# Two transformer blocks on one core: products of a quarter taken kind by kind in the blocks after each norm

## The chip, the cores and the metric

The kernel runs on one NeuronCore of a Trainium2 chip. The metric is the device time of one execution in microseconds (us), as the median of several runs. All matrix data are float32; TensorE multiplies them in its float32r format.

## What is computed

Two transformer blocks over one sequence of 256 tokens with 1024 features. Cut to what matters here:

```python
def first_block(x, mem, ...):
    h = _rmsnorm(x, norm_mix_pre)
    x = x + _rmsnorm(_mixer_sublayer(h, ...), norm_mix_post)
    h = _rmsnorm(x, norm_mem_pre)
    x = x + _rmsnorm(_memory_cross_attention(h, mem, ...), norm_mem_post)
    h = _rmsnorm(x, norm_ffn_pre)
    return x + _rmsnorm(_swiglu(h, w_gate_up, w_down), norm_ffn_post)

def second_block(x, ...):
    for layer in range(2):
        if layer == 1: shared = nsa_shared_kv(h, kv_w, ...)
        h = post_norm(h, 0.5 * swiglu(h, ...), ...)
        mix = chunked_sgu_mixer(h, ...) if layer == 0 else nsa_mixer(h, shared, ...)
        h = post_norm(h, mix, ...)
        h = post_norm(h, 0.5 * swiglu(h, ...), ...)
```

So there are five SwiGLU feed-forward parts (width 2816), three mixers, and a norm between any two of them. Each norm needs the whole row of a token, so the next product cannot begin on a token before its norm is done.

## The kernel before

**Split in two parts.** For accuracy every operand of a weight product is kept as two float32r tiles: the rounded value (high part) and what rounding left (low part). A product of an activation tile and a weight tile is three matmuls into the same PSUM bank: high by high, high by low, low by high. `product` (L632) issues them one after another, so in the profile L634, L635 and L636 are the three kinds. In the token layout the stationary operand is `st_hi` or `st_lo` (128 features by 128 tokens) and the moving operand a row of `whi` or `wlo` (512 or 256 columns).

**Weights.** They stream through a ring of three slots of 1 MB, called units, as a fixed list. SyncE issues the loads into `raw`; ScalarE copies to `whi` (L1393, semaphore `whi_ready`); VectorE subtracts to `wlo` (L1939, `wlo_ready`), GpSimd for a few units (L2638). The first two units of the program are split by halves, with `half_hi_ready` and `half_lo_ready` for the first half (L1408, L2066). TensorE counts `w_used` when a unit is done, which frees its `whi` and `wlo`.

**Activations.** The 256 tokens are two blocks of 128 (tb 0 and 1). VectorE writes the normed block by halves of 512 features (L1981, L1995 or L2030). `turn_st` (L672) waits for a half and transposes its four 128 by 128 pieces into a bank (L678); ScalarE copies the bank to `st_hi` (L1415, `hi_rounded`), and then VectorE subtracts to `st_lo` (L1961), which counts the bank's `bank_read`. Four k (128 features each) that came from one bank are called a quarter below: half of the features of one token block.

**The order around a norm.** Each engine runs its own list in the order of the program; nothing is scheduled at run time. `by_block` (L694) is the part of TensorE's list behind each norm: for each token block it takes all k of two units, so that block 0 can be multiplied while block 1 is being normed. Near the end of block 0, before its last two k, it turns the first half of block 1 (and calls `beside`); in block 1 at the same place it calls `ahead`. It waits for `wlo_ready` once per unit, which implies the high part, and for the `bank_read` of `st_lo` at each quarter. By name of the transposed tile, the norms are: mix (first one, at 12 us of the span), merged (at 160), ffn0 (at 252), b2 (at 444), ln0 (at 632), ln1 (at 778), ln2 (at 967; here the units have 256 columns and 8 k) and ln4 (at 1310). `by_block` is also used without a norm: at the tails of output projections (`tail=True`), where `ahead` turns the first half of the coming norm, and at the start of the fourth SwiGLU, `swiglu(3)`, at 1007 us, whose `beside` is `cmp_turns` (L1170).

## Time and profile before

| what | value |
|---|---|
| median of 3 runs | 1511.88 us (1511.25 to 1513.43) |
| the profiled execution | 1510.47 us |
| its span in the trace | 1508.7 us, 20416 instructions |
| TensorE | 7688 matmuls, busy 98% of the span |
| VectorE, ScalarE, GpSimd | busy 58%, 45%, 12% |
| DMA | 274.47 MB, 181 GB/s read over the span |
| mean granted TensorE clock | 0.993 |

The profiled execution took 1.8 us more than its span and is 1.4 us below the median. "Busy" is the share of the span in which an engine works on an instruction; the rows of a time line give start and duration in us, the engine, the line of the kernel, output and inputs, and in square brackets how long the engine sat idle before and which instruction ended that. A matmul's duration overlaps the next one's, so the pace is read from the distance of starts.

### The profile page before, as it was taken

How to read it: one execution, taken by the hardware profiler on the slowest of the kernel's cores; microseconds unless marked ns; L12 is line 12 of the kernel's file. 1: busy time of each engine (PE TensorE's matmuls, PEld its weight loads, DVE VectorE, ACT ScalarE, POOL GpSimd, SP SyncE). 2: the span in 40 equal slices, each digit the busy share in tenths (PEclk: the TensorE clock that was granted, in tenths of full speed). 3: DMA queues.
4: the chain of work that ended last, by engine and by line, in shares of the span. 5: the costliest groups of instructions: out<-in, count | busy, mean ns of one | idle time of the engine just before them, and what ended most of it. 6: DMA issues, size and time to landing. Idle time of an engine off the chain costs nothing.

```text
span 1508.7 us, 20416 instructions
## 1 busy us (share of the span) xinstructions
PE 1474.9 (98%) x7688; PEld 1243.8 (82%) x7688; DVE 870.1 (58%) x1030; ACT 685.9 (45%) x850; POOL 188.4 (12%) x192
## 2 busy tenths in 40 slices
PE   9999998999999999999999999999999999999997
PEld 8988796888878888789978888888888886788886
DVE  5765766545455455657665554665445677654555
ACT  5346455433444434454434344364443477444332
POOL 1074022000010000300040000300000325500000
PEclk9999998999999999999999999999999999999999
DMA  9754553855556556465566556575555440465551
GB/s 298 230 163 149 180 182 108 278 180 186 195 161 214 179 184 195 166 204 188 189 208 214 179 192 195 169 231 187 193 178 187 154 156 29 141 221 186 178 193 56
DMA packets 198875, 274.47 MB, mean 182 GB/s; under 512 B 9632, under 2 KB 158240, under 8 KB 198560
## 3 DMA queue, kind: packets, MB, share of 16 engines
q1 hardware_dynamic: 194304, 256.62, 52.7%
q0 software_dynamic: 4368, 16.78, 3.2%
q8 instruction: 40, 0.66, 0.2%
q10 hardware_dynamic: 144, 0.26, 0.0%
q14 instruction: 19, 0.16, 0.0%
HBM read 272.32 MB, written 1.31 MB: 181 GB/s over the span
## 4 chain that ended last, share of the span: by engine, by line
PE 88%; DVE 5%; ACT 3%; POOL 2%; issue 1%; DMA 0%; SPq 0%; DVEq 0%; ACTq 0%; POOLq 0%
PE ps L634 27%; PE ps L636 27%; PE ps L635 27%; PE ps L1035 1%; PE ps L678 1%; ACT whi L1393 1%; DVE wlo L1939 1%; DVE tmp L2026 1%; PE ps L1232 1%; PE ps L1107 0%; DVE stats L2014 0%; DMA raw<-in_w_in 0%; DVE tmp L2008 0%; DVE st_lo L1961 0%; DVE res L2030 0%
## 5 line engine op out<-in xcount | busy, mean ns | idle before, releaser
L1939 DVE TENSOR_TENSOR wlo<-raw,whi 128x2048 fp32r<-128x2048 f32 (+1 forms) x230 | 526.3, 2292 | 323.6 <-ACT whi L1393 322.5
L1393 ACT CAST whi<-raw 128x2048 fp32r<-128x2048 f32 (+1 forms) x241 | 456.1, 1895 | 230.6 <-PE ps L636 225.5
L634 PE MATMUL ps<-whi,st_hi 128*128 128x512 f32 (+2 forms) x1304 | 515.2, 395 | 8.5 <-DVE st_lo L1961 4.4
L636 PE MATMUL ps<-whi,st_lo 128*128 128x512 f32 (+2 forms) x1304 | 504.6, 387 | 0.0
L635 PE MATMUL ps<-wlo,st_hi 128*128 128x512 f32 (+2 forms) x1304 | 504.4, 387 | 0.0
L634 PEld LDWEIGHTS ps<-whi,st_hi 128*128 128x128 f32 (+1 forms) x1304 | 244.9, 188 | 59.8 <-DVE wlo L1939 6.7
L636 PEld LDWEIGHTS ps<-whi,st_lo 128*128 128x128 f32 (+1 forms) x1304 | 244.9, 188 | 50.7
L635 PEld LDWEIGHTS ps<-wlo,st_hi 128*128 128x128 f32 (+1 forms) x1304 | 245.3, 188 | 46.2
L634 PE MATMUL ps<-whi,hid_hi 128*128 128x512 f32 x400 | 156.1, 390 | 0.0
L636 PE MATMUL ps<-whi,hid_lo 128*128 128x512 f32 x400 | 155.9, 390 | 0.0
L635 PE MATMUL ps<-wlo,hid_hi 128*128 128x512 f32 x400 | 155.7, 389 | 0.0
L634 PE MATMUL ps<-st_hi,whi 128*128 128x256 f32 (+1 forms) x464 | 133.6, 288 | 0.0
L635 PE MATMUL ps<-st_lo,whi 128*128 128x256 f32 (+1 forms) x464 | 131.5, 284 | 0.0
L636 PE MATMUL ps<-st_hi,wlo 128*128 128x256 f32 (+1 forms) x464 | 131.5, 283 | 0.0
L2638 POOL TENSOR_TENSOR wlo<-raw,whi 128x2048 fp32r<-128x2048 f32 x11 | 50.8, 4615 | 625.5 <-ACT whi L1393 625.5
L1663 ACT CAST hid_hi<-ps 128x512 fp32r<-128x512 f32 x50 | 29.4, 587 | 188.8 <-PE ps L1035 188.8
L1653 ACT ACTIVATE silu<-ps 128x256 f32<-128x256 f32 x110 | 42.2, 384 | 150.3 <-PE ps L636 150.3
L2305 DVE TENSOR_TENSOR hid_lo<-ps,hid_hi 128x512 fp32r<-128x512 f32 x50 | 34.6, 691 | 107.6 <-ACT hid_hi L1663 107.6
L634 PEld LDWEIGHTS ps<-st_hi,whi 128*128 128x128 f32 (+1 forms) x464 | 88.8, 191 | 2.1 <-issue 1.9
L635 PEld LDWEIGHTS ps<-st_lo,whi 128*128 128x128 f32 (+1 forms) x464 | 88.8, 191 | 0.7 <-issue 0.5
L636 PEld LDWEIGHTS ps<-st_hi,wlo 128*128 128x128 f32 (+1 forms) x464 | 88.7, 191 | 0.0
L636 PEld LDWEIGHTS ps<-whi,hid_lo 128*128 128x128 f32 x400 | 75.1, 188 | 15.6
(252 smaller groups left out, 1148.8 us busy)
## 6 DMA issues: line engine op xcount, KB each, us to landing
raw<-in_ffn_w SPq DMA_DIRECT2D x264, 512.0 KB, 4.3
raw<-in_w_gate_up SPq DMA_DIRECT2D x44, 512.0 KB, 4.7
raw<-in_w_in SPq DMA_DIRECT2D x32, 512.0 KB, 5.1
raw<-in_sgu_w_in SPq DMA_DIRECT2D x32, 512.0 KB, 4.6
raw<-in_w_down SPq DMA_DIRECT2D x22, 512.0 KB, 4.1
raw<-in_sgu_w_out SPq DMA_DIRECT2D x16, 512.0 KB, 4.9
raw<-in_kv_w SPq DMA_DIRECT2D x12, 512.0 KB, 4.0
raw<-in_w_proj_attn SPq DMA_DIRECT2D x8, 512.0 KB, 4.7
```

Of the source, the lines that this page charges most:

```text
L634: pe.matmul(o, a[0], b[0], start=start, stop=False)
L635: pe.matmul(o, a[0], b[1], start=False, stop=False)
L636: return pe.matmul(o, a[1], b[0], start=False, stop=stop)
L678: mm = pe.transpose(bank(key)[:, k * P:k * P + P], src[:, tb, (4 * q + k) * P:(4 * q + k + 1) * P], ident)
L1035: mm = pe.transpose(bank(hid)[:, (2 * f + tb) * P:(2 * f + tb + 1) * P], hidden[:, tb, f * P:f * P + P], ident)
L1232: mm = pe.matmul(o.rearrange("p (a b) -> p a b", a=2), q2[r:r + 64, i, tb * P:tb * P + P], k2[r:r + 64, i // 2, :, 0:n], start=True, stop= ...
L1393: act.copy(whi[:, s, 0:n], raw[:, s, 0:n]).then_inc(whi_ready, 1)
L1653: act.activation(silu[:, tb, :], bank(("up", n, tb))[:, 0:FC], ACT.Silu).then_inc(silu_ready, 1)
L1663: act.copy(hid_hi[:, :, :].rearrange("p a b -> p (a b)"), bank(("hid", n))).then_inc(hi_rounded, 1)
L1939: dve.tensor_tensor(wlo[:, s, 0:n], raw[:, s, 0:n], whi[:, s, 0:n].bitcast(F32), ALU.subtract).then_inc(wlo_ready, 1)
L2305: dve.tensor_tensor(hid_lo[:, :, :].rearrange("p a b -> p (a b)"), bank(("hid", n)), hid_hi[:, :, :].rearrange("p a b -> p (a b)").bitcast ...
L2638: pool.tensor_tensor(wlo[:, s, 0:n], raw[:, s, 0:n], whi[:, s, 0:n].bitcast(F32), ALU.subtract).then_inc(wlo_ready, 1)
```

## The change

In `by_block` the matmuls of a quarter are grouped by kind: four high by high, four high by low, four low by high. For the first two units of the program in block 0 the groups are of two k. Before the first kind it waits for `whi_ready` (or `half_hi_ready`) and for `hi_rounded` of the activations; before the second for `wlo_ready` (or `half_lo_ready`); before the third for the `bank_read` of `st_lo`. The calls in the last quarter of a block (turning block 1, `beside`, `ahead`) come behind the high by low matmuls when the unit has 512 columns, behind the high by high ones when it has 256. `each`, which waits for the heads at the memory attention's projection, is now called ahead of each high by high matmul. Loops outside `by_block` still use `product`.

```diff
--- before.py
+++ after.py
@@ -635,12 +635,9 @@
                 pe.matmul(o, a[0], b[1], start=False, stop=False)
                 return pe.matmul(o, a[1], b[0], start=False, stop=stop)
 
-            def weights(u, kt, cols, first_half=False):
-
-                if first_half:
-                    pe.wait_ge(half_lo_ready, u + 1)
-                else:
-                    pe.wait_ge(wlo_ready, u + 1)
+            def weights(u, kt, cols):
+
+                pe.wait_ge(wlo_ready, u + 1)
                 s = u % RING
                 n = kt * cols
                 return [w[:, s, 0:n].rearrange("p (k c) -> p k c", k=kt) for w in (whi, wlo)]
@@ -695,29 +692,55 @@
 
 
 
+                def hooks(tb):
+                    if tb == 0 and st is not None:
+                        turn_st(st, src, 1, 0)
+                    if tb == 0 and beside is not None:
+                        beside()
+                    if tb == 1 and ahead is not None:
+                        ahead()
+
                 for tb in range(2):
                     if st is not None:
                         transpose_st(st, src, tb)
                     for u, kt, cols, k0, outs, keys, start, stop in parts:
-                        w = weights(u, kt, cols, first_half=u < 2 and tb == 0)
+                        s = u % RING
+                        w_hi, w_lo = [w[:, s, 0:kt * cols].rearrange("p (k c) -> p k c", k=kt) for w in (whi, wlo)]
+                        halved = u < 2 and tb == 0
                         if start:
                             room(keys[tb])
-                        for k in range(kt):
-                            if (u, k) == (parts[-1][0], kt - 2):
-                                if tb == 0 and st is not None:
-                                    turn_st(st, src, 1, 0)
-                                if tb == 0 and beside is not None:
-                                    beside()
-                                if tb == 1 and ahead is not None:
-                                    ahead()
-                            if u < 2 and (tb, k) == (0, 2):
+                        step = 2 if halved else 4
+                        for k1 in range(0, kt, step):
+                            ks = range(k1, k1 + step)
+                            q = (k0 + k1) // 4
+                            final = (u, k1) == (parts[-1][0], kt - step)
+                            t = slice(tb * P, tb * P + P)
+                            if halved and k1 == 0:
+                                pe.wait_ge(half_hi_ready, u + 1)
+                            else:
+                                pe.wait_ge(whi_ready, u + 1)
+                            if st is not None:
+                                pe.wait_ge(hi_rounded, split_no["st", st, tb, q] + 1)
+                            for k in ks:
+                                if each is not None and (tb, u) == (0, parts[0][0]):
+                                    each(k)
+                                pe.matmul(outs[tb], st_hi[:, k0 + k, t], w_hi[:, k, :], start=start and k == 0,
+                                          stop=False)
+                            if halved and k1 == 0:
+                                pe.wait_ge(half_lo_ready, u + 1)
+                            else:
                                 pe.wait_ge(wlo_ready, u + 1)
-                            if st is not None and (k0 + k) % 4 == 0:
-                                pe.wait_ge(*read(("st", st, tb, (k0 + k) // 4)))
-                            if each is not None and (tb, u) == (0, parts[0][0]):
-                                each(k)
-                            mm = product(outs[tb], [x[:, k0 + k, tb * P:tb * P + P] for x in (st_hi, st_lo)],
-                                         [x[:, k, :] for x in w], start and k == 0, stop and k == kt - 1)
+                            if final and cols == 256:
+                                hooks(tb)
+                            for k in ks:
+                                pe.matmul(outs[tb], st_hi[:, k0 + k, t], w_lo[:, k, :], start=False, stop=False)
+                            if final and cols == 512:
+                                hooks(tb)
+                            if st is not None:
+                                pe.wait_ge(*read(("st", st, tb, q)))
+                            for k in ks:
+                                mm = pe.matmul(outs[tb], st_lo[:, k0 + k, t], w_hi[:, k, :], start=False,
+                                               stop=stop and k == kt - 1)
                         if tb == 1:
                             mm.then_inc(w_used, 1)
                         elif stop and keys[0] != keys[1]:
```

TensorE's list at the norm called merged, before. L678 is `turn_st`; the rows begin behind the two turns of block 0, and `bank_read6` is the first quarter of `st_lo`, `bank_read0` the output bank:

```order
L678 MATMUL ps<-con,tmp 128x128 [waits bank_read7,xn_ready]
L678 MATMUL ps<-con,tmp 128x128 x3
L634 MATMUL ps<-whi,st_hi 128x512 [waits bank_read6,bank_read0,wlo_ready]
L635 MATMUL ps<-wlo,st_hi 128x512
L636 MATMUL ps<-whi,st_lo 128x512
L634 MATMUL ps<-whi,st_hi 128x512
L635 MATMUL ps<-wlo,st_hi 128x512
L636 MATMUL ps<-whi,st_lo 128x512
```

The same place in the changed kernel, down to the turn of block 1's first half (L675 is `turn_st` there; L727, L736 and L742 are the three kinds):

```order
L675 MATMUL ps<-con,tmp 128x128 [waits bank_read7,xn_ready]
L675 MATMUL ps<-con,tmp 128x128 x3
L727 MATMUL ps<-whi,st_hi 128x512 [waits hi_rounded,whi_ready,bank_read0]
L727 MATMUL ps<-whi,st_hi 128x512 x3
L736 MATMUL ps<-wlo,st_hi 128x512 [waits wlo_ready]
L736 MATMUL ps<-wlo,st_hi 128x512 x3
L742 MATMUL ps<-whi,st_lo 128x512 [waits bank_read6]
...
L736 MATMUL ps<-wlo,st_hi 128x512 [waits wlo_ready]
L736 MATMUL ps<-wlo,st_hi 128x512 x3
L675 MATMUL ps<-con,tmp 128x128 [waits bank_read6,xn_ready]
L675 MATMUL ps<-con,tmp 128x128 x3
L742 MATMUL ps<-whi,st_lo 128x512 [waits bank_read7]
```

The first matmul no longer waits for `wlo_ready` and `bank_read6`; eight matmuls stand ahead of the wait for `st_lo`. The turn of block 1 has four matmuls of block 0 behind it, where it had six.

TensorE's list at the second unit of `swiglu(3)`, before and then after (L1170 and L1193 are `cmp_turns`):

```order
L634 MATMUL ps<-whi,st_hi 128x512 [waits wlo_ready]
L635 MATMUL ps<-wlo,st_hi 128x512
L636 MATMUL ps<-whi,st_lo 128x512
L634 MATMUL ps<-whi,st_hi 128x512
L635 MATMUL ps<-wlo,st_hi 128x512
L636 MATMUL ps<-whi,st_lo 128x512
L1170 MATMUL ps<-con,big 128x60 [waits bank_read1,bank_read0]
```

```order
L727 MATMUL ps<-whi,st_hi 128x512 [waits whi_ready]
L727 MATMUL ps<-whi,st_hi 128x512 x3
L736 MATMUL ps<-wlo,st_hi 128x512 [waits wlo_ready]
L736 MATMUL ps<-wlo,st_hi 128x512 x3
L1193 MATMUL ps<-con,big 128x60 [waits bank_read1,bank_read0]
```

Four matmuls of the second unit moved ahead of the wait for its low part. The lists of VectorE, ScalarE, GpSimd and SyncE hold the same instructions in the same order.

## Rows read from the trace of the kernel before

**Rows 1.** The page: busy time of the engines.

```profile
PE 1474.9 (98%) x7688; PEld 1243.8 (82%) x7688; DVE 870.1 (58%) x1030; ACT 685.9 (45%) x850; POOL 188.4 (12%) x192
```

**Rows 2.** Who TensorE waited for: us in total, times, longest.

```profile
PE ps L634 <- DVE st_lo L1961: 4.4, 7, 1.4
PE ps L634 <- DVE wlo L1939: 3.7, 4, 1.8
PE ps L678 <- DVE res L2030: 2.0, 4, 0.8
```

**Rows 3.** Time line, TensorE at a steady pace: the first and last of eleven matmuls.

```profile
157.05 0.39 PE L634 MATMUL ps<-whi,st_hi 128*128 128x512 f32 x1
...
159.32 0.39 PE L635 MATMUL ps<-wlo,st_hi 128*128 128x512 f32 x1
```

**Rows 4.** Time line at merged: the turns, the parts' makers, the first product.

```profile
159.78 0.60 PE L678 MATMUL ps<-con,tmp 128*128 128x128 f32 x4
160.13 0.47 PE L634 MATMUL ps<-whi,st_hi 128*128 128x512 f32 x1
160.48 0.57 ACT L1415 CAST st_hi<-ps 128x512 fp32r<-128x512 f32 x1
160.60 2.29 DVE L1939 TENSOR_TENSOR wlo<-raw,whi 128x2048 fp32r<-128x2048 f32 x1 [1.55 <-ACT whi L1393]
161.59 0.60 PE L678 MATMUL ps<-con,tmp 128*128 128x128 f32 x4
162.81 1.28 DVE L1961 TENSOR_TENSOR st_lo<-ps,st_hi 128x512 fp32r<-128x512 f32 x2
163.64 0.47 PE L634 MATMUL ps<-whi,st_hi 128*128 128x512 f32 x1 [1.45 <-DVE st_lo L1961]
```

**Rows 5.** Time line at ln0: first product of block 0, turn of block 1.

```profile
634.00 0.47 PE L634 MATMUL ps<-whi,st_hi 128*128 128x512 f32 x1 [0.36 <-DVE st_lo L1961]
...
639.26 0.66 PE L678 MATMUL ps<-con,res 128*128 128x128 f32 x4 [0.82 <-DVE res L2030]
```

**Rows 6.** Time line: turns of block 1 at b2 (and a product ahead), ln1, ln4.

```profile
448.95 0.50 PE L634 MATMUL ps<-whi,st_hi 128*128 128x512 f32 x1 [0.28 <-DVE wlo L1939]
...
450.81 0.66 PE L678 MATMUL ps<-con,res 128*128 128x128 f32 x4 [0.20 <-DVE res L1995]
...
785.46 0.66 PE L678 MATMUL ps<-con,res 128*128 128x128 f32 x4 [0.47 <-DVE res L2030]
...
1317.56 0.66 PE L678 MATMUL ps<-con,res 128*128 128x128 f32 x4 [0.47 <-DVE res L2030]
```

**Rows 7.** Time line at ln2: first products of block 0 and, last row, block 1.

```profile
968.65 0.36 PE L634 MATMUL ps<-whi,st_hi 128*128 128x256 f32 x1 [0.36 <-DVE st_lo L1961]
...
976.05 0.36 PE L634 MATMUL ps<-whi,st_hi 128*128 128x256 f32 x1 [0.34 <-DVE st_lo L1961]
```

**Rows 8.** Time line, second unit of swiglu(3): high part, low part, TensorE.

```profile
1007.61 1.91 ACT L1393 CAST whi<-raw 128x2048 fp32r<-128x2048 f32 x1
1009.55 2.29 DVE L1939 TENSOR_TENSOR wlo<-raw,whi 128x2048 fp32r<-128x2048 f32 x1 [3.12 <-ACT whi L1393]
1011.89 0.50 PE L634 MATMUL ps<-whi,st_hi 128*128 128x512 f32 x1 [1.84 <-DVE wlo L1939]
```

**Rows 9.** Time line at ffn0: turns of block 0, first product, turn of block 1.

```profile
252.31 1.32 PE L678 MATMUL ps<-con,tmp 128*128 128x128 f32 x8 [0.55 <-DVE tmp L1981]
254.62 0.65 PE L634 MATMUL ps<-whi,st_hi 128*128 128x512 f32 x1 [0.99 <-DVE st_lo L1961]
262.53 0.66 PE L678 MATMUL ps<-con,tmp 128*128 128x128 f32 x4 [1.93 <-DVE tmp L1981]
```

**Rows 10.** Windows: stretch: length, busy by engine, PEclk, DMA share, GB/s.

```profile
254.00:259.00 5.00, 4.38 (x12) 3.51 (x13) 5.00 (x6) 0.25 (x1) 0.34 (x1) 0.66 0.05 13
1012.00:1016.00 4.00, 4.00 (x13) 2.77 (x14) 2.29 (x1) 3.91 (x8) 0.00 (x0) 0.57 0.80 264
```

**Rows 11.** Time line at mix: the first product behind the turn of block 1.

```profile
17.52 0.50 PE L634 MATMUL ps<-whi,st_hi 128*128 128x512 f32 x1 [0.37 <-DVE wlo L2066]
```

## The prediction

> **What bounds the kernel now.** I read the page's busy times first: TensorE works in 1474.9 of 1508.7 us [rows 1]. The change adds and removes no matmul, so all it can win is in the 34 us in which TensorE stands still, and in its clock. The table of who waited for whom comes next: before a first product behind a norm TensorE waited 4.4 us in seven places for `st_lo` and 3.7 us in four for `wlo`, and before a turn 2.0 us in four for VectorE's norm [rows 2]. Then I read the time line at each of the places and asked which wait ends last there. The pace to count with is (159.32 - 157.05) / 10 = 0.227 us for one 512-column matmul [rows 3]; a 256-column one follows the next after 0.12 us by the same reading.
>
> **Merged.** Block 0's second turn starts at 161.59. Where nothing waits, a product starts 0.35 us after a turn (159.78 to 160.13), so it could start at 161.95; it starts at 163.64 [rows 4]. It needed `st_lo`, and VectorE could not make that before it had done the next unit's `wlo` (160.60 to 162.89); the first half of `st_lo` came at 162.81 + 1.28 / 2, about 163.5. The high parts were there: the first `st_hi` in the changed kernel at 160.48 + 0.57 + 0.45 = 161.5, since its turn now stands two matmuls later (0.45). So high by high starts at 161.95, and high by low after 0.91 at 162.87, with both `wlo` there. Low by high would start at 163.78, and `st_lo` is there since 163.5. The whole wait goes: 163.64 - 161.95 = **1.69 us**. Later waits do not eat it, as VectorE's next work behind this point follows TensorE's turns of block 1.
>
> **The norms with block 1 late: ffn0, b2, ln0, ln1, ln4.** Here filling the first wait is not the gain. At ln0 the first product can start earlier than 634.00: by the 0.36 us idle shown, by starts 0.6, as at merged 1.45 shown was 1.69. The 20 matmuls then end near 638.0, and TensorE waits at the turn of block 1, which VectorE lets go at 639.26 whatever TensorE does before [rows 5]. The earlier start only lengthens that wait. What does gain is the turn's new place: four matmuls of block 0 remain behind it in place of six, so two are done during the wait: 2 x 0.227 = **0.45 us**, provided TensorE stands at least that long there. b2, ffn0, ln1 and ln4 have the same form [rows 6, 9]; the wait shown is 0.20 at b2, but 0.28 for `wlo` at 448.95 and the like of ln0's first wait are now added to it, so it is long enough. At ln1 and ln4 `ahead` in the tail is also two matmuls later, by which the turn of block 0 slips 0.1 to 0.2 us and VectorE's chain about 0.07: 0.38 each. Sum: 3 x 0.45 + 2 x 0.38 = **2.1 us**.
>
> **ln2 (256 columns).** The same holds, but here eight small matmuls stay behind the turn in place of six: 2 x 0.12 = 0.24 lost. In return block 1's first product no longer waits for `st_lo` until 976.05 [rows 7]: the turn pair ends at about 975.7. Net **0.35 us**.
>
> **swiglu(3).** The second unit's high part is ready at 1007.61 + 1.91 = 1009.52, its low part at 1011.84, and TensorE stands from about 1010.05 to 1011.89 [rows 8]. Four high by high matmuls now go there: 4 x 0.227 = **0.91 us**.
>
> **mix.** Its first product starts about 0.7 us earlier, but block 1 is held by the second unit's `wlo` until 17.52 [rows 11]. Before, six matmuls and one more turn stood behind that; now it is four matmuls and two turns. Two matmuls (0.45) against one turn with its switch (0.46): **0**. The tail at the memory attention waits for all four heads before any low part; the last head's arrives within the fourth matmul: 0, within 0.2 either way.
>
> **Added waits** on TensorE's queue are on semaphores already reached in most places. The eleven matmuls of rows 3 cross from one unit to the next, with its wait, at an even pace, so I price them at nothing; bound from above, an idle piece of 0.20 us as the smallest one shown at b2 [rows 6], at ten places, would be 2 us.
>
> **The clock.** The trace has two short stretches at the lower level, 1.2 GHz (a granted share of 0.50), that the change touches. After idle pieces of 0.55 and 0.99 us around eight transposes [rows 9] the clock fell at 254.9 and came back before 259; lost is 1 - PEclk over the window, 5 x 0.34 = 1.7 us of work [rows 10]. At ffn0 this cost nothing, since TensorE still reached the turn 1.93 us early. The other: idle 1.84 us [rows 8], then a clock of 0.57 over 4 us [rows 10], 4 x 0.43 = 1.7 us, all of it on the path. With high by high in the gap, idle shrinks to about 1.0 us there, less than pieces that did not bring the clock down (1.45 in rows 4, 1.93 in rows 9), so I count **1.7 us won**. At ffn0 the opposite happens. High by high follows the turns at once (252.31 + 1.32, about 253.7), 20 matmuls at 0.227 end at about 258.3, and TensorE then stands in one piece until 262.53: some 4 us where it was 1.93. That is over twice anything here that left the clock high. I count a fall behind it, now on the path: at least 0, at most two stretches (3.4); I take **1.4 us lost**, near one stretch, part of which passes while TensorE is still waiting.
>
> For that place the Trainium skill, "TensorE: Matmul & The Clock Gate", section "Why this matters for your kernels", warns that idle gaps between bursts of matmuls bring the clock down to the half rate. That speaks against a change that gathers small gaps into one. No row here has a gap of this length before a norm's turn.
>
> **Sum.** 1.69 + 2.1 + 0.35 + 0.91 = 5.1 us, plus 1.7, minus 1.4: 5.4 us. The profiled execution of 1510.47 would become 1505.1. It is 1.4 us faster than the median of its runs; against the median, 1511.88 - 5.4 = **1506.5 us**. A difference under 0.2% (3.0 us) can't be told from none here.
>
> **Rivals.**
> 1. *The clock takes back a part.* ffn0 costs two stretches, or `swiglu(3)` falls all the same. 5.1 - 3.4 = 1.7 to 5.1 - 1.4 = 3.7: 1508.2 to 1510.2. For it: where a gap falls in time shifts with every us gained ahead of it. Against it: five of the gaps stay at or below 1.2 us.
> 2. *The norms give it all back.* If VectorE's norm itself slips when the turn comes later (it waits for `st_lo` of block 0, so for TensorE's turns), the 2.1 us are gone and 3.3 us remain: 1508.6. Against it: at ln0 block 0's turns stand outside the moved part.
> 3. *Slower: the gathered gaps drop the clock at every norm.* TensorE now stands 0.7 to 1.2 us in one piece at b2, ln0, ln1 and ln4 before the turn of block 1, and 4 us at ffn0. A stretch of 1.7 us at each is 8.5 us against 5.1: 3.4 us slower than before, 1515.3. It decides from the fourth fall on. Against it: gaps of 1.45 and 1.93 us without a fall.
> 4. *The turn's new place hurts nothing and ffn0 keeps its clock:* 1511.88 - 6.8 = 1505.1, and to 1504 if TensorE's start at mix also tells.
> 5. *The order does nothing*, as if TensorE still waited for everything: excluded by its list, where the waits stand ahead of their own kinds.
>
> **How the numbers follow.** Forecast 58% (its own range 1505.5 to 1508.2), rival 1 17%, rival 2 12%, rival 3 4%, rival 4 9%. Faster by over 0.2% is below 1508.86: the forecast, rival 4, about a fifth of rival 1 and half of rival 2, 0.76. Slower by over 0.2% is rival 3, 0.04. The rest, 0.20, is within. The range takes in rivals 1, 2 and 4 nearly whole: 1504.2 to 1510.3.
>
> **What would show it.** In the changed profile no product behind a turn waits for `st_lo`: 4.4 us becomes under 0.5. The waits of turns for the norm grow from 2.0 us in four places to about 4 us (and near 4 us at ffn0 alone). After each turn of block 1 four low by high matmuls follow. The product at merged starts 0.36 us after the turn. PEclk at `swiglu(3)` stays at 1.00, and behind ffn0's turn it shows 0.5 for some us. The forecast is wrong if `st_hi` is late behind the turns, if VectorE's norms end at another distance from the last output bank than now, or if the 0.227 us pace of matmuls changes with their grouping.

## The result, and the profile after

| | before | changed |
|---|---|---|
| median of 5 runs each | 1511.79 us (1511.25 to 1513.43) | 1503.99 us (1503.10 to 1504.95) |
| ratio, 95% interval | 1 | 0.9949 (0.9937 to 0.9961) |
| the profiled execution | 1510.47 us | 1504.95 us |
| its span | 1508.7 us | 1503.2 us |

The changed kernel is 7.8 us faster by medians, 5.5 us by the two profiled executions. The forecast was 5.4 us: near for the profiled executions, by luck as shown below, and too small for the medians. The page of the changed kernel, busy times, against [rows 1]:

```profile
PE 1469.6 (98%) x7688; PEld 1241.3 (83%) x7688; DVE 870.1 (58%) x1030; ACT 686.0 (46%) x850; POOL 188.3 (13%) x192
```

Who TensorE waited for in the changed kernel (us in total, times, longest), against [rows 2]:

```profile
PE ps L675 <- DVE tmp L2004: 4.4, 2, 3.8
PE ps L675 <- DVE res L2053: 2.5, 3, 1.0
PE ps L634 <- DVE wlo L1962: 1.6, 2, 1.3
PE ps L736 <- DVE wlo L2089: 1.3, 2, 0.8
PE ps L736 <- DVE wlo L1962: 0.9, 1, 0.9
...
PE ps L727 <- ACT st_hi L1438: 0.3, 1, 0.3
PE ps L727 <- DVE st_lo L2284: 0.2, 1, 0.2
```

L1984 now makes `st_lo` behind the norms, and no row names it: seven waits, 4.4 us, are gone. What grew is turns (L675) waiting for the norm, the longest 3.8 us, at ffn0. (L2284 is at the memory attention.) Over the four norms whose turns follow below, the waits before the turn of block 1 add up to 3.15 us, where they were 1.96.

Time line of the changed kernel at merged, TensorE and then VectorE, against [rows 4]:

```profile
162.98 0.60 PE L675 MATMUL ps<-con,tmp 128*128 128x128 f32 x4
163.34 1.17 PE L727 MATMUL ps<-whi,st_hi 128*128 128x512 f32 x4
164.35 1.08 PE L736 MATMUL ps<-wlo,st_hi 128*128 128x512 f32 x4
165.27 1.07 PE L742 MATMUL ps<-whi,st_lo 128*128 128x512 f32 x4
...
161.98 2.29 DVE L1962 TENSOR_TENSOR wlo<-raw,whi 128x2048 fp32r<-128x2048 f32 x1 [1.55 <-ACT whi L1416]
164.19 1.28 DVE L1984 TENSOR_TENSOR st_lo<-ps,st_hi 128x512 fp32r<-128x512 f32 x2
```

The product follows the turn after 0.36 us, where it was 2.05. Its first low by high matmul comes at 165.27; half of `st_lo` is there at 164.19 + 1.28 / 2 = 164.83.

Time line of the changed kernel, turns of block 1 at b2, ln0, ln1 and ln4, against [rows 5, 6]:

```profile
451.32 0.66 PE L675 MATMUL ps<-con,res 128*128 128x128 f32 x4 [0.67 <-DVE res L2018]
...
639.33 0.66 PE L675 MATMUL ps<-con,res 128*128 128x128 f32 x4 [1.05 <-DVE res L2053]
...
785.09 0.66 PE L675 MATMUL ps<-con,res 128*128 128x128 f32 x4 [0.71 <-DVE res L2053]
...
1312.46 0.66 PE L675 MATMUL ps<-con,res 128*128 128x128 f32 x4 [0.72 <-DVE res L2053]
```

Each wait is longer than before (0.20, 0.82, 0.47, 0.47), and the time won is behind it: at ln0 block 1's second turn stands 640.75 - 639.33 = 1.42 us after the first, before 641.14 - 639.26 = 1.88, so two matmuls (0.46) are gone.

Time line of the changed kernel at ln2 (block 0's second turn, block 1's first product) and at the second unit of swiglu(3), against [rows 7, 8]:

```profile
966.85 0.60 PE L675 MATMUL ps<-con,res 128*128 128x128 f32 x4
...
974.88 0.72 PE L727 MATMUL ps<-whi,st_hi 128*128 128x256 f32 x4
...
1010.73 1.19 PE L736 MATMUL ps<-wlo,st_hi 128*128 128x512 f32 x4 [0.94 <-DVE wlo L1962]
```

From turn to product at ln2 it is 8.03 us, before 976.05 - 967.69 = 8.36. At swiglu(3) the wait for the low part is 0.94 us, where it was 1.84.

Time line of the changed kernel at ffn0, against [rows 9]:

```profile
253.23 1.16 PE L727 MATMUL ps<-whi,st_hi 128*128 128x512 f32 x4 [0.27 <-ACT st_hi L1438]
...
261.86 0.66 PE L675 MATMUL ps<-con,tmp 128*128 128x128 f32 x4 [3.83 <-DVE tmp L2004]
262.28 1.54 PE L742 MATMUL ps<-whi,st_lo 128*128 128x512 f32 x4
263.62 1.05 PE L675 MATMUL ps<-con,tmp 128*128 128x128 f32 x4
264.32 2.06 PE L727 MATMUL ps<-whi,st_hi 128*128 128x512 f32 x4
```

The gap before the turn is 3.83 us, where it was 1.93, and behind it four high by high matmuls take 2.06 us; at merged, at full rate, four took 1.17. Here the rule of the Trainium skill, "TensorE: Matmul & The Clock Gate", section "Why this matters for your kernels", that the prediction weighed is borne out: the 3.83 us gap is followed by half the clock.

Windows of the changed kernel (length, busy by engine, PEclk, DMA share, GB/s) at the memory attention, ffn0, swiglu(3) and the second attention:

```profile
230.00:244.00 14.00, 9.36 (x38) 7.14 (x37) 8.79 (x12) 6.32 (x15) 3.78 (x2) 0.88 0.25 75
252.00:272.00 20.00, 15.90 (x69) 12.51 (x68) 12.16 (x16) 9.98 (x17) 5.07 (x11) 0.91 0.61 210
1008.00:1020.00 12.00, 11.06 (x50) 8.57 (x50) 5.67 (x5) 8.59 (x13) 0.00 (x0) 1.00 0.77 257
1220.00:1240.00 20.00, 18.50 (x161) 17.08 (x160) 15.13 (x63) 14.59 (x51) 10.36 (x16) 1.00 0.28 95
```

The same windows of the kernel before:

```profile
230.00:244.00 14.00, 10.04 (x35) 7.83 (x35) 8.24 (x12) 6.25 (x16) 3.78 (x1) 0.76 0.23 75
252.00:272.00 20.00, 16.76 (x72) 13.23 (x73) 13.33 (x17) 10.65 (x19) 5.07 (x11) 0.91 0.58 208
1008.00:1020.00 12.00, 10.15 (x39) 7.50 (x39) 5.01 (x3) 7.75 (x12) 0.00 (x0) 0.86 0.87 286
1220.00:1240.00 20.00, 19.27 (x153) 17.27 (x154) 14.19 (x58) 13.89 (x40) 8.70 (x14) 0.91 0.47 156
```

One stretch at 1.2 GHz is 1 - PEclk over the window: 14 x 0.12, 20 x 0.09, 12 x 0.14, each about 1.7 us of work. So the trace of before holds 2, 1, 1 and 1 stretches in the four windows, the changed one 1, 1, 0 and 0. The last, inside the second attention, was in no term of the forecast. Its place, before and then changed:

```profile
1228.68 1.97 PE L1251 MATMUL ps<-big 64*128 64x16 f32 x32 [0.73 <-ACT big L1840]
1230.45 2.50 PE L1232 MATMUL ps<-big 64*128 64x256 f32 x8
```

```profile
1225.11 1.97 PE L1274 MATMUL ps<-big 64*128 64x16 f32 x32 [0.73 <-ACT big L1863]
1226.89 1.58 PE L1255 MATMUL ps<-big 64*128 64x256 f32 x8
```

The idle piece ahead of it, 0.73 us, and the 32 small matmuls are the same in both kernels; only before did the eight matmuls behind them take 2.50 us in place of 1.58.

**The difference in pieces.** Three marks in the same work: merged's last turn, VectorE's `wlo` for swiglu(3)'s second unit, block 1's turn at ln4.

| stretch | before | changed | difference | by forecast |
|---|---|---|---|---|
| start to merged's turn | 161.59 | 162.98 | +1.39 | 0 |
| to the `wlo` of swiglu(3) | 847.96 | 845.40 | -2.56 | -1.69 - 0.45 x 3 - 0.38 - 0.35 + 1.4 = -2.4 |
| to ln4's turn | 308.01 | 304.08 | -3.93 | -0.91 - 1.7 = -2.6 |
| rest | 191.1 | 190.7 | -0.4 | -0.38 |

The sum is -5.5. Two things that the forecast does not have nearly cancel in it: merged's turn came 1.39 us later, and 1.3 us more went between swiglu(3) and ln4. The later start is the first transfer's, as the first copy of a weight's high part shows, before and then changed:

```profile
8.79 1.05 ACT L1408 CAST whi<-raw 128x1024 fp32r<-128x1024 f32 x1 [3.04 <-DMA raw<-in_w_in]
```

```profile
10.04 1.05 ACT L1431 CAST whi<-raw 128x1024 fp32r<-128x1024 f32 x1 [4.50 <-DMA raw<-in_w_in]
```

From this copy to merged's turn it is 152.80 us before and 152.94 changed; to mix's last turn (19.01 and 20.32) 10.22 and 10.28. So mix gives nothing, as forecast.

### The profile page after: what moved, and what is told of

Its sections match the earlier page's. It is cut to its first block, busy times and chain, and to the rows that moved or that the text cites. A ratio compares the mean times of both kernels' runs of the same rounds, so it can differ in the third digit from the quotient of the medians.

```text
span 1503.2 us, 20422 instructions
## 1 busy us (share of the span) xinstructions
PE 1469.6 (98%) x7688; PEld 1241.3 (83%) x7688; DVE 870.1 (58%) x1030; ACT 686.0 (46%) x850; POOL 188.3 (13%) x192
## 4 chain that ended last, share of the span: by engine, by line
PE 88%; DVE 5%; ACT 3%; POOL 2%; issue 1%; DMA 1%; SPq 0%; DVEq 0%; ACTq 0%; POOLq 0%
PE ps L634 25%; PE ps L636 25%; PE ps L635 25%; PE ps L742 3%; PE ps L736 3%; PE ps L727 2%; PE ps L1058 1%; PE ps L675 1%; ACT whi L1416 1%; DVE wlo L1962 1%; DVE tmp L2049 1%; PE ps L1255 1%; DMA raw<-in_w_in 1%; PE ps L1130 0%; DVE stats L2037 0%
## 5 line engine op out<-in xcount | busy, mean ns | idle before, releaser
L634 PE MATMUL ps<-whi,st_hi 128*128 128x512 f32 (+1 forms) x1064 | 419.6, 394 | 1.6 <-DVE wlo L1962 1.6
L636 PE MATMUL ps<-whi,st_lo 128*128 128x512 f32 (+1 forms) x1064 | 413.2, 388 | 0.0
L635 PE MATMUL ps<-wlo,st_hi 128*128 128x512 f32 (+1 forms) x1064 | 412.7, 388 | 0.0
L636 PEld LDWEIGHTS ps<-whi,st_lo 128*128 128x128 f32 (+1 forms) x1064 | 198.8, 187 | 41.9
L634 PEld LDWEIGHTS ps<-whi,st_hi 128*128 128x128 f32 (+1 forms) x1064 | 198.9, 187 | 41.2 <-DVE wlo L1962 2.1
L635 PEld LDWEIGHTS ps<-wlo,st_hi 128*128 128x128 f32 (+1 forms) x1064 | 199.2, 187 | 38.9
```

The costliest lines, as they stand in the source:

```text
L634: pe.matmul(o, a[0], b[0], start=start, stop=False)
L635: pe.matmul(o, a[0], b[1], start=False, stop=False)
L636: return pe.matmul(o, a[1], b[0], start=False, stop=stop)
```

## The experiments

Theory A: the waits are worth what the sum says, and what goes beyond it is clock. Theory B: the new order saves waits that the sum missed. Each comparison is with runs of the kernel before on the same chip, whose medians were 1510.91 to 1511.45 in the four series.

### Both kernels once more, and the turn's place

`before_again`, `before_third` and `before_look4` are the kernel before, `after_again` and `after_look3` the changed one, with no edit.

> The kernel before, unchanged, timed and profiled once more. Theory A (the missing 2.4 us of the forecast lie in stretches at the lower TensorE clock that the old order brings in most executions, in the attention of the second block among others): this trace too shows a mean granted clock near 0.993 and a stretch at 0.5 somewhere in 1218 to 1262 us, and 1.5 to 3 us more low-clock loss than the changed kernel. Theory B (chance of one execution): the stretch is absent here or elsewhere, the loss differs from 0.007 x 1508 us by over 2 us.

> The changed kernel, unchanged, timed and profiled once more: ratio 0.9949 as on record, within 0.0006. Theory A: clock 0.995 to 0.996 and no stretch at 0.5 in the second attention, as in the first profile; TensorE's start as late as in the first profile or up to 1.3 us earlier (a transfer at the start). Theory B: the low stretches lie at other places, and only ffn0's remains in both.

> The kernel before, one more execution for the stretches at the lower clock alone. Theory A: 3 to 4 stretches on the path (two in a row at 234 to 241, one at swiglu(3), one at 1231), where the changed kernel has two, at 235 and behind ffn0's turn. Theory B: 2 to 3.

> The kernel before, one more execution. Theory A: stretches at the lower clock on the path: three to four, among them swiglu(3)'s.

> The changed kernel, one more execution. Theory A: two or three stretches on the path: one at 235, one behind ffn0's turn, perhaps one in the second attention; none at swiglu(3).

`hooks6` puts the calls back to where six matmuls remain (at merged and in `ahead` and `beside` too):

```diff
+                                if final and cols == 512 and step == 4 and k == k1 + 2:
+                                    hooks(tb)
...
-                            if final and cols == 512:
+                            if final and cols == 512 and step == 2:
```

> The changed kernel with the turn of block 1 back where six matmuls of block 0 remain behind it (but at mix). Theory 1 (the late turn gives 0.45 us at each of ffn0, b2, ln0, ln1, ln4, since VectorE sets when the turn can go): 5 x 0.45 = 2.2 us slower than the changed kernel, 0.9964 of before, and the starts of block 1's turns at these norms unchanged against the norm's own work. Theory 2 (the gain of the norms is the earlier first product): within 0.5 us of the changed kernel.

`late2` goes the other way, two matmuls behind the turn at the five norms:

```diff
+                            late = tb == 0 and st in LATE
-                            if final and cols == 512:
+                            if final and cols == 512 and not late:
...
+                                if final and cols == 512 and late and k == k1 + 2:
+                                    hooks(tb)
```

> The changed kernel with the turn of block 1 another two matmuls later at ffn0, b2, ln0, ln1 and ln4, so that two low by high matmuls stay behind it. TensorE waits 0.65 us or more at each of these turns, st_hi is ready 1.3 us after the turn and two matmuls with the second turn last 1.3. Theory 1: another 0.4 to 0.45 us at each, 2.1 us faster than the changed kernel, 0.9942 of before, with waits at the turns 0.45 us shorter. Theory 2 (st_hi becomes the wait behind the turns): gain under 0.5 us, with waits of L727 for ScalarE's L1438 copy.

`before_turn4` is the old order with the turn two matmuls later at the same norms:

```diff
+                            if last4:
+                                pe.matmul(outs[tb], a[0], w[0][:, k, :], start=False, stop=False)
+                                pe.matmul(outs[tb], a[0], w[1][:, k, :], start=False, stop=False)
+                                turn_st(st, src, 1, 0)
+                                mm = pe.matmul(outs[tb], a[1], w[0][:, k, :], start=False, stop=False)
+                                continue
```

> The kernel before, its order of products kept, with only the turn of block 1 moved to where four matmuls of block 0 remain behind it, at ffn0, b2, ln0, ln1 and ln4. Theory 1 (the late turn pays only together with the order by kind, since a first product that waits for the low part of block 1 comes 2.1 us after the turn, while four matmuls and the second turn last 1.75): the starts of block 1's first product gain 0.1 to 0.2 us at each norm, 0.4 to 0.8 us in all, ratio 0.9996, with a new wait for st_lo of about 0.2 there. Theory 2 (the place of the turn alone gives the norms' gain): 2 us faster than before, 0.9986.

| kernel | median us | ratio, 95% interval | profiled |
|---|---|---|---|
| before_again | 1511.15 | 0.9998 (0.9988 to 1.0007) | 1508.47 |
| before_third | | | 1510.24 |
| before_look4 | | | 1511.76 |
| after_again | 1503.48 | 0.9956 (0.9944 to 0.9968) | 1503.24 |
| after_look3 | | | 1504.06 |
| hooks6 | 1508.62 | 0.9984 (0.9975 to 0.9993) | 1507.04 |
| late2 | 1502.46 | 0.9939 (0.9926 to 0.9952) | 1506.27 |
| before_turn4 | 1509.93 | 0.9993 (0.9984 to 1.0002) | 1510.39 |

The trace of `before_again` missed its theory A in part: its mean granted clock is 0.997, with the stretch in the second attention but none at ffn0 and `swiglu(3)`. `before_third` and `before_look4` have all those that A expected. The ratio of `after_again` is 0.0007 from the first one, where 0.0006 was forecast.

Block 1's turn at ln0, of `hooks6` and of `late2`:

```profile
639.12 0.66 PE L675 MATMUL ps<-con,res 128*128 128x128 f32 x4 [1.50 <-DVE res L2055]
```

```profile
640.20 0.66 PE L675 MATMUL ps<-con,res 128*128 128x128 f32 x4 [0.60 <-DVE res L2058]
```

With six, four and two behind, TensorE waits 1.50, 1.05 and 0.60 us there: 0.45 per pair, as if VectorE alone set when the turn goes. From this turn to the next one it is 1.89, 1.42 and 0.95 us. In `before_turn4`:

```profile
640.12 0.66 PE L678 MATMUL ps<-con,res 128*128 128x128 f32 x4 [0.35 <-DVE res L2039]
```

```profile
642.27 0.47 PE L634 MATMUL ps<-whi,st_hi 128*128 128x512 f32 x1
```

There the wait fell from 0.82 to 0.35 and the second turn came 0.47 us sooner, but block 1's first product still needs `st_lo`: it starts 2.15 us behind the first turn, where it was 641.49 - 639.26 = 2.23. In `hooks6`, with the new order and the old place, it is 641.36 - 639.12 = 2.24, with both changes 641.11 - 639.33 = 1.78. So neither wins alone, 0.08 and 0 us; together they give 0.45. By medians `before_turn4` shows no gain that can be told, and `late2` is 1.0 us below `after_again`, where 2.1 was forecast; the intervals overlap, so its gain is shown in the trace alone.

`hooks6` against `after_again` is 5.1 us by medians, where the turns explain 2.1. Its trace has a stretch at 1.2 GHz in the second attention that `after_again` lacks. Clock fits the rest: 8 of its 11 executions have a mean granted clock of 0.993, none of the twelve of the changed kernel is below 0.994 (see the last table on the clock).

### The clock at ffn0, the memory attention and swiglu(3)

`fill_ffn0` puts matmuls whose result nothing reads into the new gap; `fill_mem` does it in the gap of the memory attention, `before_fill3` in that of the kernel before at `swiglu(3)`.

```diff
+                    if tb == 0 and st in ("ffn0",):
+                        room(parts[0][5][1])
+                        for _ in range(15):
+                            pe.matmul(parts[0][4][1], st_hi[:, 0, 0:P], whi[:, parts[-1][0] % RING, 0:512],
+                                      start=True, stop=True)
```

> The changed kernel with 15 extra matmuls of 512 columns into the still free bank of block 1, ahead of the turn of block 1 at ffn0 only; their results are overwritten. They take 15 x 0.227 = 3.4 us of the 3.83 us that TensorE stands there. Theory 1 (the gathered gap brings the clock down behind it): clock 1.00 behind that turn, 1.3 us (0.8 to 1.7) faster than the changed kernel. Theory 2 (the clock would come down anyway, or the extra matmuls delay the turn): within 0.4 us of it, or slower.

```diff
+            for _ in range(14):
+                pe.matmul(ps[:, 6, :], st_hi[:, 0, 0:P], st_hi[:, 0:2, :].rearrange("p a b -> p (a b)"),
+                          start=True, stop=True)
```

> The changed kernel with 14 extra matmuls (3.2 us, results never read) in the gap of 3.87 us in the memory attention, ahead of the turn of its third head. Theory 1 (this gap brings the clock down at 234 to 238 us or longer in every execution): no stretch at the lower clock there, 0.4 to 1.7 us faster than the changed kernel. Theory 2 (the stretch is hidden behind VectorE's chain there): within 0.4 us.

```diff
+                        if tb == 0 and u == first["ffn", 3] + 1 and cols == 512 and kt == 4:
+                            room(keys[1])
+                            for _ in range(8):
+                                pe.matmul(outs[1], st_hi[:, 0, 0:P], whi[:, (u - 1) % RING, 0:512],
+                                          start=True, stop=True)
```

> The kernel before with 8 extra matmuls (1.8 us, results overwritten) in the gap of 1.84 us ahead of the second unit of swiglu(3). Theory A (this gap brings the clock down in most executions, which the changed kernel's shorter gap does not): clock 1.00 there, median 1 to 1.7 us faster than before. Theory B (it did so by chance in the one execution that was profiled first): within 0.5 us of before.

`fill_ffn0`, time line at the gap and window:

```profile
256.71 3.56 PE L699 MATMUL ps<-whi,st_hi 128*128 128x512 f32 x15
260.71 0.66 PE L675 MATMUL ps<-con,tmp 128*128 128x128 f32 x4 [0.44 <-DVE tmp L2009]
...
262.47 1.17 PE L732 MATMUL ps<-whi,st_hi 128*128 128x512 f32 x4
...
252.00:272.00 20.00, 19.49 (x89) 15.96 (x90) 13.93 (x15) 8.84 (x13) 4.59 (x9) 1.00 0.68 234
```

The clock stays and four matmuls take 1.17 us in place of 2.06. From ffn0's turn to b2's second (from 262.53 to 444.75 before) this kernel is 0.47 us shorter than before and the changed one 1.18 longer: the fall costs 1.65 us against an execution in which ffn0's stretch was hidden, the turn's place gives 0.47. Its median is 1504.07 (ratio 0.9956, 0.9943 to 0.9969), that of `after_again` 1503.48: no gain can be told there, though its profiled execution took 1501.50. That one had a mean granted clock of 0.997, its four others 0.994 to 0.996: they lost more clock somewhere, and where no trace shows.

`fill_mem`: median 1502.95 (0.9948, 0.9935 to 0.9962). Its window at the memory attention:

```profile
230.00:244.00 14.00, 12.49 (x57) 9.59 (x56) 9.61 (x13) 6.25 (x15) 4.04 (x2) 1.00 0.23 75
```

From block 0's turns at 206 us to those at 252, which hold both stretches, `fill_mem` takes 44.35 us, the changed kernel 45.72 with one stretch, the kernel before 46.12 with two. The gap was in the trace of before, with both stretches behind it:

```profile
234.80 2.27 PE L937 MATMUL ps<-con,big 128*128 128x128 f32 x8 [3.87 <-DVE big L2255]
```

`before_fill3`: median 1509.04 (0.9989, 0.9980 to 0.9998), PEclk 1.00 at `swiglu(3)` and 0.83 in the window of ffn0, two stretches where `before` had one. It is 1.9 us faster than before (0.3 to 3.0), where theory A said 1 to 1.7 and B under 0.5: A fits, and B's 0.5 lies within the interval.

The old order too can have its gap at ffn0 in one piece: where the clock does not fall ahead of it, TensorE stands 3.53 us in `before_again`, 3.07 in `before_turn4`, 3.55 in `before_fill3`. The first two had no fall behind it, the third had two stretches there and took 2.6 us longer than `before` from ffn0's turn to b2's.

### The old order back in one place

`old_merged` and `old_swiglu3` are the changed kernel with the old loop at one place, `st == "merged"` or `swiglu(3)`'s call:

```diff
+                        if st == "merged":
+                            pe.wait_ge(wlo_ready, u + 1)
+                            for k in range(kt):
...
+                                mm = product(outs[tb], [x[:, k0 + k, tb * P:tb * P + P] for x in (st_hi, st_lo)],
+                                             [w_hi[:, k, :], w_lo[:, k, :]], start and k == 0, stop and k == kt - 1)
```

> The changed kernel with the old order of products (and the old place of the turn) behind the norm called merged alone. Theory 1 (the whole wait for st_lo there was won and kept): 1.7 us slower than the changed kernel, and TensorE waits 1.4 us for L1984's st_lo in the first product there. Theory 2 (later waits take back a part): under 1 us slower.

> The changed kernel with the old order of products at the start of swiglu(3) alone. Theory A: 0.9 us for four matmuls plus the clock's 1.7 us in most executions, 2 to 2.6 us slower than the changed kernel, 0.9970 of before. Theory B: 0.9 to 1.3 us slower.

`old_merged` at merged, the turn and the product:

```profile
161.86 0.60 PE L675 MATMUL ps<-con,tmp 128*128 128x128 f32 x4
163.90 0.47 PE L634 MATMUL ps<-whi,st_hi 128*128 128x512 f32 x1 [1.44 <-DVE st_lo L1998]
```

2.04 us from turn to product, 0.36 with the change: the term of 1.69 is shown. Medians 1506.12 (0.9967, 0.9955 to 0.9978) and, for `old_swiglu3`, 1505.70 (0.9968, 0.9956 to 0.9979): 2.6 and 2.2 us over `after_again`, for terms of 1.69 and of 0.91 with or without a stretch (the trace of `old_swiglu3` has none at `swiglu(3)`, and one in the second attention). The excess of `old_merged` over its term, 0.9 us, is within the noise.

### Where the clock falls, over all traces

PEclk of the four windows in the profiled executions:

| kernel | 230:244 | 252:272 | 1008:1020 | 1220:1240 |
|---|---|---|---|---|
| before | 0.76 | 0.91 | 0.86 | 0.91 |
| before_again | 0.88 | 1.00 | 1.00 | 0.91 |
| before_third | 0.76 | 0.91 | 0.86 | 0.91 |
| before_look4 | 0.76 | 0.91 | 0.86 | 0.91 |
| before_turn4 | 0.76 | 1.00 | 0.86 | 0.91 |
| before_fill3 | 0.76 | 0.83 | 1.00 | 1.00 |
| after | 0.88 | 0.91 | 1.00 | 1.00 |
| after_again | 0.88 | 0.91 | 1.00 | 1.00 |
| after_look3 | 0.76 | 0.91 | 1.00 | 1.00 |
| hooks6 | 0.88 | 0.91 | 1.00 | 0.91 |
| late2 | 0.76 | 0.83 | 1.00 | 0.91 |
| old_merged | 0.76 | 0.83 | 1.00 | 1.00 |
| old_swiglu3 | 0.88 | 0.91 | 1.00 | 0.91 |
| fill_mem | 1.00 | 0.91 | 1.00 | 0.91 |
| fill_ffn0 | 0.88 | 1.00 | 1.00 | 1.00 |
| before_filled | 1.00 | 0.91 | 1.00 | 1.00 |
| after_filled | 1.00 | 1.00 | 1.00 | 0.91 |
| best | 1.00 | 1.00 | 1.00 | 1.00 |

The same kernel with the same gaps does not always have the fall. Here `before_again`'s gap at `swiglu(3)`:

```profile
1012.13 0.50 PE L634 MATMUL ps<-whi,st_hi 128*128 128x512 f32 x1 [1.83 <-DVE wlo L1939]
...
1008.00:1020.00 12.00, 10.17 (x47) 7.79 (x46) 5.01 (x3) 9.11 (x12) 0.00 (x0) 1.00 0.90 296
```

1.83 us idle, no fall; in `before` 1.84 and a fall. What a stretch costs on the path is read between the last two marks, the `wlo` of swiglu(3) and ln4's turn: 308.0 us in `before`, `before_third` and `before_look4` (both stretches), 306.5 in `before_again` (one, in the second attention), 305.7 in `hooks6` and `late2` (new order, that stretch alone), 304.1 in `after`, `after_again`, `after_look3` and `fill_ffn0` (none). So 1.5 us for the one at `swiglu(3)`, 1.6 for the one in the second attention, and 305.7 to 306.5 leaves 0.8 for the gap filled by high by high. Without any stretch the old order takes 305.0 (`before_fill3`, `before_filled`): 0.9 over the new one's 304.1, as forecast (0.91).

Every execution but the first five of before has a mean granted clock on record, also those without a trace. Medians at the same clock, us (number of executions):

| granted clock | before | changed |
|---|---|---|
| 0.992 | 1512.93 (18) | |
| 0.993 | 1511.37 (8) | |
| 0.994 | 1511.05 (43) | 1505.96 (2) |
| 0.995 | 1510.25 (1) | 1504.06 (3) |
| 0.996 | 1507.85 (5) | 1503.24 (7) |
| 0.997 | 1508.28 (10) | |

Within a kernel an execution is about 0.96 us longer per 0.001 of clock lost (a fit over all kernels here). Brought to one clock by it, which is an estimate, the changed kernel is 5.4 us faster than before (95% interval 5.0 to 5.8); `old_merged` is 1.8 us slower than the changed kernel, `old_swiglu3` 1.2, `hooks6` 2.5, `late2` 1.6 faster, and `fill_ffn0` within 0.3. The means of the clock, 0.9940 and 0.9954, are worth another 1.4 us.

### Both kernels with their gaps filled

To part A from B: matmuls that nothing reads in the gaps of both kernels (14 at the memory attention; 7 at ffn0 and 8 at `swiglu(3)` before, 15 at ffn0 after). By A the two then differ by the waits alone, 5.1 to 5.3 us; by B by 7 or more. The 7 leave 1.98 us of idle at ffn0 in `before_filled`, since the clock had not fallen ahead of that gap; a stretch follows the turn there. `after_filled` has one stretch too, in the second attention.

> The kernel before with its three large gaps filled by extra matmuls whose results are never read: 14 in the memory attention (3.87 us), 7 ahead of the turn of block 1 at ffn0 (1.93 us), 8 at swiglu(3) (1.84 us). Theory A (what the medians show beyond the sum of waits is TensorE's clock): about 1507, since one stretch or two at 236 and one at swiglu(3) go, and 5.3 us (the sum of the waits alone, 1.65 + 3 x 0.46 + 2 x 0.5 + 0.33 + 0.91) above the changed kernel with its gaps filled. Theory B (some wait was missed): the difference to that kernel stays at 7 to 8 us.

> The changed kernel with 14 extra matmuls in the memory attention's gap and 15 at ffn0. Theory A: about 1502, 1.5 to 2.5 us below the changed kernel, and 5.3 us below the filled kernel of before. Theory B: 7 to 8 us below that.

| kernel | median us | ratio, 95% interval | profiled |
|---|---|---|---|
| before_filled | 1505.96 | 0.9971 (0.9957 to 0.9984) | 1507.91 |
| after_filled | 1502.04 | 0.9941 (0.9926 to 0.9955) | 1502.12 |

Filling alone makes the kernel before 5.5 us faster and the changed one 1.4 us; the difference shrinks from 7.7 to 3.9 us by medians (5.8 in the profiled executions). The mean granted clocks are alike, 0.9977 and 0.9978. B's 7 to 8 us are out. The 3.9 us lie below A's 5.3, not above; by means the difference is 4.6. So no wait of 2 us was missed, and what the change gives beyond some 5 us it gives through the clock.

### A version that beats both

`best` is `late2` with 13 matmuls in ffn0's gap and 14 in the memory attention's.

> The changed kernel with the turn of block 1 two matmuls later at five norms, 13 extra matmuls in ffn0's gap and 14 in the memory attention's. Theory 1: 2.1 + 1.6 + about 1 = 4.7 us faster than the changed kernel, about 1499.2 us, ratio 0.9922 of before; the only low-clock stretch left may be that of the second attention. Theory 2 (extra matmuls delay what follows or only move the stretches): not faster than the kernel with the later turn alone (1502.5).

Median 1500.42 us (1499.42 to 1501.13), ratio 0.9933 (0.9919 to 0.9946). Who TensorE waited for, and the window of ffn0:

```profile
PE ps L970 <- DVE big L2291: 1.5, 3, 0.7
...
PE ps L675 <- DVE res L2066: 1.1, 3, 0.6
PE ps L675 <- DVE tmp L2017: 1.0, 2, 0.6
...
252.00:272.00 20.00, 19.56 (x90) 15.89 (x90) 13.14 (x14) 8.41 (x12) 4.07 (x8) 1.00 0.74 246
```

All four windows have a PEclk of 1.00 in this execution. `best` is 3.6 us below the changed kernel's 1503.99 (3.1 below `after_again`), where 4.7 was forecast.

## Why the prediction was right and where it was wrong

- **Merged, 1.69 us:** right. 2.05 became 0.36, and `old_merged` brings 2.04 back (2.6 us slower by medians, 1.8 at the same clock).
- **The turn's place, 0.45 each at ffn0, b2 and ln0, 0.38 at ln1 and ln4:** right, and so was the reason, that the earlier first product is worth nothing without it (`hooks6`). Shown from turn to turn were 0.46 at b2 and ln0, 0.47 at ffn0 (in `fill_ffn0`, without the clock), 0.46 at ln1 (1.42 where it was 1.88) and 0.45 at ln4 (1.43 where it was 1.88). The 0.07 taken off for `ahead` lies ahead of these turns; from ln0's last turn to ln1's it is 145.76 us, before 146.20, so 0.44 was won and the 0.07 did not show. What the forecast left out is that in the old order the later turn is eaten by the wait for `st_lo` behind it (`before_turn4`). The waits at the turns became 3.15 us and not about 4: at ln0 the first product came 0.60 us earlier behind its turn, the later place of the next turn took most of that, and the wait grew by 0.23.
- **ln2, 0.35:** right; the trace has 0.33.
- **swiglu(3), 0.91 and 1.7 of clock:** the wait fell from 1.84 to 0.94 us. The stretch was worth 1.5 on the path, in the executions that had it; with the old order and the gap left open four traces of six had it, with the new one none.
- **ffn0, 1.4 lost:** right in kind and nearly in size, 1.65 against the profiled execution. The row that bears most on it, 3.87 us of idle in the memory attention with a fall behind it, was in the trace and not used. Rival 4 is out, though its 1504 is the figure nearest to the result: ffn0 did not keep its clock. Rival 1 falls too: in the three traces of the changed kernel the clock took back one stretch at ffn0 and none at `swiglu(3)`. Rivals 2 and 3 are out: from block 0's second turn to block 1's first it is 6.22 us before and 6.21 changed at ln0, so VectorE's norm did not slip, and gaps of 0.67 to 1.05 us before these turns brought no fall.
- **Added waits, nothing:** right; the pace in groups is (165.27 - 164.35) / 4 = 0.23 us.

**The step that failed is the clock's term**, "the trace has two short stretches at the lower level that the change touches". It counted the stretches next to edited work as the one trace had them, 1.7 won less 1.4 lost, 0.3 us net. A third one, in the second attention at 1231 to 1235, 210 us behind the last edit ahead of it, was in all four traces of the unchanged kernel before and in none of the three of the changed one: 1.6 us. At the memory attention the kernel before had two stretches in three traces of four, the changed one in one of three: 46.12 against 45.72, 0.4 us of the difference between the profiled executions. Waits and clock together then are 1.69 + 0.46 x 5 + 0.33 + 0.9 = 5.2, plus 1.5 at swiglu(3), 1.6 and 0.4, less 1.65 at ffn0: 7.1 us, of which the clock is 1.9. Over the 97 executions of both kernels the clock is worth 1.4 us (an estimate, from the table by clock).

**That 5.4 matched the profiled executions (5.5) was luck.** The changed one began 1.39 us late, and merged's turn shows how this varies: 161.59, 162.62, 162.24 and 162.93 us in the four traces of the kernel before, 162.98, 162.15 and 162.42 in those of the changed one. Before's profiled execution had the earliest start of them, which fits its place 1.4 us under the median; in its clock, 0.993, it was an ordinary one. If starts spread alike in both kernels, the 7.1 us tell in full in the medians: 1511.8 - 7.1 = 1504.7, and 1503.99 was measured. The remaining 0.7 is within the interval of the ratio (5.9 to 9.5 us), and chance of five runs fits it: the later 85 executions of before have a median of 1511.11, all twelve of the changed kernel one of 1503.93, 7.2 us apart.

**Open:** whether the new order makes the stretch in the second attention rarer. Four of four against none of three speaks for it; but over all kernels with the new order around the norms five traces of eleven have it (`hooks6`, `late2`, `old_swiglu3`, `fill_mem` and `after_filled`), and with the old order five of seven (not `before_fill3` and `before_filled`). What decides there, no run here shows; the idle piece ahead of it is 0.73 us with and without the fall.

## What to carry to other kernels

Where a norm on another engine sets when the next block can be turned, an earlier first product wins nothing by itself; what wins is fewer matmuls left behind the turn, and only if the next block's first product does not wait for a part that comes later still. Grouping by kind pays in full only where the missing low part was the last thing waited for. Before trusting a sum to a fraction of a per cent, take several traces of the unchanged kernel: which stretches at half clock it has, and when its first transfers are through, each moved single executions here about as much as the largest wait that was won (1.4 to 1.6 us, against 1.69). Where every execution has a granted clock on record, compare executions of the same clock.

## What was not expected of the hardware

- The same gap (1.83 and 1.84 us) at the same place was followed by a fall of the clock in four traces with the old order there and not in two others; an idle piece of 3.53 us at ffn0 was followed by none in `before_again`, one of 3.55 by two stretches in `before_fill3`.
- Matmuls that nobody reads, put in the place of idle time, made the kernel before 5.5 us faster (1511.45 to 1505.96) with no other edit.
- The start of the program, until merged's last turn, differed by 1.4 us over the seven traces of the two kernels, with the landing of the first transfer.
